# Hybrid diffusion layer on one core: the conditioning product on weights split into high and low parts, with the opening reordered

## What is computed

```python
def mixer_layer(x, mod, rms_g, w_in, b_in, ..., attend):
    shift, scale, gate = jnp.split(mod, 3, axis=-1)
    h = rmsnorm(x, rms_g) * (1 + scale) + shift
    q, k, v, z_a, glu, z_b, gates = jnp.split(h @ w_in + b_in, PROJ_SPLITS, axis=-1)
    ...
# context tokens:  mod = silu(c_ctx) @ w_ada + b_ada
# latent tokens:   mod = silu(c) @ w_ada + b_ada       w_ada is 1024 x 3072
```

## Time and profile before

| what | value |
|---|---|
| median of 3 runs | 1916.28 us (1915.32 to 1918.64) |
| profiled execution, its own time | 1918.94 us |
| profiled execution, span of the core | 1917.1 us |
| TensorE busy | 1861.3 us, 97% of the span |
| VectorE, ScalarE busy | 1018.0 us, 540.8 us |
| first product of `h @ w_in` starts | 45.85 us from the span's start |
| first product of the second chunk starts | 70.45 us |

### The profile page before, as it was taken

The page is one execution under the profiler, slowest core; times in us unless marked ns, Lnnn a source line. Parts: engine busy times, 40 slices in busy tenths (PEclk is TensorE's granted clock), DMA queues, the critical chain, the costliest instruction groups (busy, mean ns, idle before and its releaser), DMA issues.

```text
span 1917.1 us, 27200 instructions
## 1 busy us (share of the span) xinstructions
PE 1861.3 (97%) x10707; PEld 1566.2 (82%) x10707; DVE 1018.0 (53%) x1713; ACT 540.8 (28%) x1053; POOL 123.8 (6%) x221
## 2 busy tenths in 40 slices
PE   7999999999999999999999999989999999999998
PEld 1788899988888888888888888878887888878886
DVE  2554512111188348807852894656667555554444
ACT  2641101021111111211111115656667322221221
POOL 0000000000000000000000014222230000000000
PEclk9999999999999999999999999999999999999999
DMA  8614423143022112202220176878884766573421
GB/s 279 197 58 159 154 72 130 50 140 114 11 90 78 58 39 80 80 28 69 88 69 28 58 169 146 185 157 178 163 164 132 230 206 202 157 256 119 156 99 55
DMA packets 212042, 235.09 MB, mean 123 GB/s; under 512 B 47707, under 2 KB 158155, under 8 KB 208715
## 3 DMA queue, kind: packets, MB, share of 16 engines
q1 hardware_dynamic: 211656, 233.24, 41.7%
q10 hardware_dynamic: 259, 0.11, 0.0%
HBM read 152.52 MB, written 80.78 MB: 122 GB/s over the span
## 4 chain that ended last, share of the span: by engine, by line
PE 88%; DMA 3%; issue 2%; DVE 2%; SPq 2%; ACT 2%; POOL 1%; POOLq 0%; DVEq 0%; ACTq 0%
PE banks L765 17%; PE banks L767 17%; PE banks L766 17%; PE banks L1145 4%; PE banks L1652 3%; PE banks L1654 3%; PE banks L1653 3%; PE banks L1624 3%; PE banks L1626 3%; PE banks L1625 3%; PE banks L1112 2%; PE banks L760 2%; PE banks L761 2%; PE banks L762 2%; PE banks L1117 1%
## 5 line engine op out<-in xcount | busy, mean ns | idle before, releaser
L765 PE MATMUL banks<-h_hi,w_hi 128*128 128x512 f32 (+1 forms) x1600 | 593.0, 371 | 3.1 <-DVE w_lo L550 1.9
L767 PE MATMUL banks<-h_hi,w_lo 128*128 128x512 f32 (+1 forms) x1600 | 589.4, 368 | 0.0
L766 PE MATMUL banks<-h_lo,w_hi 128*128 128x512 f32 (+1 forms) x1600 | 589.2, 368 | 0.0
L706 DVE SCALAR_TENSOR_TENSOR conv_acc<-glu_out,taps,conv_acc 128x773 f32<-128x773 f32 x360 | 371.7, 1032 | 12.2
L765 PEld LDWEIGHTS banks<-h_hi,w_hi 128*128 128x128 f32 x1600 | 302.0, 189 | 56.5 <-DVE w_lo L550 2.8
L767 PEld LDWEIGHTS banks<-h_hi,w_lo 128*128 128x128 f32 x1600 | 301.7, 189 | 50.6
L766 PEld LDWEIGHTS banks<-h_lo,w_hi 128*128 128x128 f32 x1600 | 301.9, 189 | 49.1
L490 ACT ACTIVATE out_stage<-banks,param_cols 128x512 f32<-128x512 f32 (+1 forms) x120 | 77.0, 647 | 442.4 <-PE banks L767 436.3
L1251 ACT ACTIVATE probs<-scores,stat 128x640 f32<-128x640 f32 (+2 forms) x128 | 106.8, 834 | 65.7 <-DVE stat L1176 64.8
L1624 PE MATMUL banks<-y_hi,wp_hi 128*128 128x512 f32 (+1 forms) x320 | 120.8, 377 | 0.6 <-DVE y_lo L1797 0.5
L1626 PE MATMUL banks<-y_hi,wp_lo 128*128 128x512 f32 (+1 forms) x320 | 118.7, 371 | 0.0
(11 more groups left out here) (155 smaller groups left out, 2419.2 us busy)
## 6 DMA issues: line engine op xcount, KB each, us to landing
proj<-out_stage SPq DMA_DIRECT2D x96, 256.0 KB, 2.0
w_raw<-in_w_in SPq DMA_DIRECT2D x44, 512.0 KB, 4.0
gates_in<-proj SPq DMA_DIRECT2D x64, 256.0 KB, 3.1
k_hi<-k_hi_rows SPq DMA_DIRECT2D x16, 640.0 KB, 13.9
k_lo<-k_lo_rows SPq DMA_DIRECT2D x16, 640.0 KB, 16.2
w_ada<-in_w_ada SPq DMA_DIRECT2D x8, 1024.0 KB, 11.2
x_rows<-in_x_sample SPq DMA_DIRECT2D x4, 2048.0 KB, 11.5
x_out<-in_x_sample SPq DMA_DIRECT2D x16, 512.0 KB, 3.7
```

Source lines behind the costliest of these rows:

```text
L706: op = dve.scalar_tensor_tensor(dst, src, tap, dst, ALU.mult, ALU.add)
L765: pe.matmul(out, w_hi[:, s, k], h_hi[c][:, k], start=first, stop=False)
L766: pe.matmul(out, w_hi[:, s, k], h_lo[c][:, k], start=False, stop=False)
L767: op = pe.matmul(out, w_lo[:, s, k], h_hi[c][:, k], start=False, stop=last)
```

## The change

The conditioning product is done on split operands. The 16 quarters of the columns (numbered q = 0 to 15; a quarter is four pieces of 128 rows by 256 columns) are each rounded by ScalarE (`ada_high`) and the remainder is made by VectorE in place (`ada_low`). The stationary operand becomes four columns: the high and the low part of the two vectors (`silu_hl`). Each piece takes two products of 256 columns, one with the high and one with the low part of the weights, both into the same four rows of the result. `turn_row` then folds the four rows into two while it transposes, by a product with a 4x2 matrix `fold` in place of the identity. `row_of` moves from VectorE to ScalarE.

```diff
         load_ada(0)
+        load_x(0)
         load_ada(1)
-        load_x(0)
+        load_w(sp, 0)
         load_ada(2)
-        load_w(sp, 0)
+        load_w(sp, 1)
         load_ada(3)
-        load_w(sp, 1)
         load_w(sp, 2)
         load_x(1)
...
+        def ada_high(q):
+            i, h, kh = q // 4, q // 2 % 2, q % 2
+            act.wait_ge(ada_in[q // 2], 16)
+            if q >= 4:
+                act.wait_ge(ada_done, q - 3)
+            act.activation(wada_hi[:, q % 4], wada[i][:, h, 4 * kh:4 * kh + 4], ACT.Copy).then_inc(ada_hid, 1)
+
+        def row_of(i):
+            act.wait_ge(ada_done, 4 * i + 4)
+            if i >= 2:
+                act.wait_ge(ada_mm, i - 1)
+            act.activation(ada_row[:, i % 2], ps_sum[i % 2], ACT.Copy).then_inc(ada_out, 1)
...
+        def ada_low(q):
+            i, h, k = q // 4, q // 2 % 2, slice(4 * (q % 2), 4 * (q % 2) + 4)
+            dve.wait_ge(ada_hid, q + 1)
+            dve.tensor_tensor(wada_lo[i][:, h, k], wada[i][:, h, k], wada_hi[:, q % 4].bitcast(F32), ALU.subtract).then_inc(ada_lod, 1)
...
-            for kc in kcs:
-                last = pe.matmul(ps_sum[i % 2], sc[:, kc], wada[i][:, :, kc], start=(kc == 0), stop=(kc == KC - 1))
+            for kh in range(2):
+                q = 4 * i + 2 * h + kh
+                pe.wait_ge(ada_lod, q + 1)
+                for k in range(4):
+                    kc = 4 * kh + k
+                    pe.matmul(out, silu_hl[:, kc], wada_hi[:, q % 4, k], start=(kc == 0), stop=False)
+                    last = pe.matmul(out, silu_hl[:, kc], wada_lo[i][:, h, kc], start=False, stop=(kc == KC - 1))
+                last.then_inc(ada_done, 1)
...
+        both(0)
...
+        turn_row(0)
+        pe.wait_ge(cols_out, 2)
+        for s in range(3):
+            turn(s)
+        both(1)
+        turn_row(1)
+        step(0, [0])
+        turn(3)
+        step(1, [0])
+        turn(4)
+        step(2, [0])
+        step(3, [0])
+        both(2)
+        for s in range(4):
+            step(s, [1])
+        turn_row(2)
+        turn(5)
+        ada_products(3, 0)
+        turn(6)
+        step(4, [0, 1])
+        ada_products(3, 1)
+        step(5, [0, 1])
+        turn_row(3)
+        turn(7)
+        for s in range(6):
+            step(s, [2])
+        step(6, [0, 1, 2])
+        step(7, [0, 1])
```

More of the change, by code:

```diff
@@ L490, in evict @@
                 act.activation(ostg[:, s, 0:w], src, func, bias=bias_of(kind, col)).then_inc(ev_act, 1)
+        for q in range(4):
+            ada_high(q)
+        row_of(0)
         squares(0)
+        ada_high(4)
+        ada_high(5)
         high(0)
[L494 to L496 removed]
+        ada_high(6)
+        ada_high(7)
+        modulate(0)
+        modulate(1)
+        row_of(1)
+        ada_high(8)
+        ada_high(9)
+        modulate(2)
+        modulate(3)
+        high(1)
+        ada_high(10)
+        ada_high(11)
+        row_of(2)
+        ada_high(12)
+        ada_high(13)
+        modulate(4)
+        modulate(5)
+        ada_high(14)
+        ada_high(15)
         high(2)
[L498 to L499 removed]
+        row_of(3)
+        modulate(6)
+        modulate(7)
         squares(1)
[L501 removed]
+        s = KC
         for i, upto in enumerate(TURNED_BY):
@@ L578, in front_dve @@
         coefficients(0)
-        row_of(1)
-        coefficients(1)
-        normalize(0)
-        row_of(2)
-        coefficients(2)
[L584 to L588, removed]
+        ada_low(4)
+        normalize(0)
+        ada_low(5)
+        low(0)
+        ada_low(6)
+        ada_low(7)
+        split(0)
+        split(1)
+        coefficients(1)
+        ada_low(8)
+        ada_low(9)
+        split(2)
+        split(3)
+        low(1)
+        ada_low(10)
+        ada_low(11)
+        coefficients(2)
+        ada_low(12)
+        ada_low(13)
+        split(4)
+        split(5)
+        ada_low(14)
+        ada_low(15)
         low(2)
-        split(3)
-        split(4)
         coefficients(3)
-        s = 5
+        split(6)
+        split(7)
+        normalize(1)
+        s = KC
         for i, upto in enumerate(TURNED_BY):
@@ L809, in front_pe, with both @@
                 products(u, i % KC)
+        def both(i):
+            ada_products(i, 0)
+            ada_products(i, 1)
+        both(0)
+        pe.wait_ge(rows_in, 16 * 7)
+        pe.transpose(ps_rows, rows[0:R_C, :], cst.ident[0:R_C, 0:R_C]).then_inc(turned, 1)
+        pe.transpose(ps_taps, taps[0:4 * TAPS, :], cst.ident[0:4 * TAPS, 0:4 * TAPS]).then_inc(turned, 1)
+        turn_row(0)
[26 more added lines that the diff above has]
+        step(7, [0, 1])
+        s = KC
+        for i, upto in enumerate(TURNED_BY):
+            if i < KC - 1:
+                continue
+            while s < upto:
+                turn(s)
+                s += 1
+            if i == KC - 1:
+                step(i, [2])
+            else:
+                step(i, range(3 * (i // KC), 3 * (i // KC) + 3))
         pe.wait_ge(lo_done, len(STEPS))
```

78 lines of the change are left out of this document (30 added, 48 removed).

## The result

| | before | changed |
|---|---|---|
| median | 1917.84 us (1914.42 to 1921.08, 20 runs) | 1921.99 us (1916.61 to 1925.26, 20 runs) |
| ratio, 95% interval | 1 | 1.0023 [1.0016, 1.0029] |
| profiled execution, span (own time) | 1917.1 us (1918.94) | 1919.1 us (1920.85) |
| TensorE busy | 1861.3 us | 1849.9 us |
| first product of `h @ w_in` | 45.85 us | 35.63 us |

The kernel is slower by 0.23% by the ratio (4.4 us on 1917.84), and by 4.15 us between the two medians. TensorE is busy for 11.4 us less and starts the projection 10.2 us sooner, and the second chunk still comes later. Turn 12 is the best mark: by then each queue holds the same instructions in both kernels, and nothing of the opening is left. It starts 76.52 - 72.62 = 3.90 us later.

What follows compares the result with a forecast made beforehand. TensorE bounds the kernel; the change moves only the second chunk's first product. At full clock 14.6 us saved are lost to waits, sum 0; clock terms +4.6, rounded to +4.5, on 1916.3 give 1920.8 us, range 1914.5 to 1926.

Steps and rivals of the forecast that it cites:

- three clock terms: TensorE's low level before turn 0 (+1.5 us), between 33 and 39 (+1.6), before turn 8 (+1.5); sum +4.6.
- Rows at 17.3 and the 5.4 us: Opening transfers: token rows move ahead of 2.1 MB of weights, 5.4 us, and land at 17.3 instead of 22.7.
- Turn 0 at 27.1: Opening on TensorE: factors at 23.5, subtraction 4 ends at 24.3, normalizing takes 2.7 us, so turn 0 at 27.1.
- Four-column products at 0.12 us: TensorE's quarters: 256-column products 0.12 us from start to start, 16 quarters 15.2 us against 29.8 before.
- the subtraction at 1.17: VectorE's 16 subtractions: about 1.17 us each from start to start, 18.7 us more before step 8.
- the plain rate: Rival on TensorE: four-column products take 0.215 us, +9 us, 1925 with the clock on top; chance 0.07.
- a cheap subtraction: Rival on VectorE: subtraction 0.9 us or less, path 2.2 to 2.9 us shorter, 1913.4 to 1914; chance 0.12.
- First product of `h @ w_in` at 34.0: TensorE after VectorE's first gapless run and the row copy: projection starts at 34.0 against 45.85, 11.9 us earlier.
- Quarters 8 to 11, `turn_row(2)`, the run of subtractions: Relay: 32 products end at 43.75, `turn_row(2)` at 46.9, coefficients at 47.3, VectorE's gapless 6.9 us to 54.2.
- Squares of the second chunk at 58.8: ScalarE after the last products, `turn_row(3)`, coefficients and `modulate` 6 and 7: the squares start only at 58.8.
- Point 6: Second chunk: squares to factors 6.2 us, normalized by 67.7; TensorE waits 2.8 for turn 8; step 8 at 70.5.
- `turn_row` 0.4 us: TensorE in the relay: each `turn_row` step takes 0.35 to 0.40 us; the 4x2 `fold` was costed at nothing.

Runs made afterwards that it cites:

- e6: Kernel before with only its transfers reissued in the changed kernel's order, token rows ahead of 2.1 MB of weights; ratio to the kernel before 1.0013.
- e5: Changed kernel with transfers issued in the order of the kernel before, token rows behind the second conditioning weights; one execution, 1926.86 us.
- e4: Changed kernel plus 64 unused products of 256 columns on TensorE between `turn_row(0)` and turn 0; ratio to the kernel before 1.0019.
- e8: Changed kernel with all edits of e7 plus the 64 unused products of e4; ratio to the kernel before 0.9993.
- e2: Changed kernel with evictions of units 0 and 1 moved right behind the second chunk's squares on ScalarE; ratio to the kernel before 1.0007.
- e1: Changed kernel with `turn_row` again four transposes of the first two rows, the vectors' low-part rows left out; ratio to the kernel before 1.0011.
- e7: Changed kernel with both edits of e9, `turn_row` transposing all four rows and VectorE adding the halves; median 1914.39 us, ratio to the kernel before 0.9982.
- e3: Changed kernel with two of the second chunk's four squares before the last row copy and two behind it; ratio to the kernel before 1.0001.
- e9: Changed kernel with the squares moved as in e3 and the evictions as in e2; ratio to the kernel before 1.0000.

## Why the prediction was right, and where it was not

The forecast was 1920.8 us against 1916.28, a ratio of 1.0024, and slower as the likelier sign; measured are 1.0023 and 1921.99 us. The 1916.28 was the median of three runs; over twenty it is 1917.84, so the +4.5 us of the forecast stand against +4.15 between medians. The frame held: the gain of the early start is lost again in a relay over VectorE and ScalarE, and the shift stands before turn 12. That the number came so near is in good part luck: of three clock terms only the first is in the profile, and two terms that the prediction did not have, the fold and the evictions, are as large as the two that are missing.

- *Rows at 17.3 and the 5.4 us.* Held. Squares start at 16.90 right behind the row copy, without a wait for the rows. In e6, where they wait for the rows alone, they start at 16.79 and not 22.71, and e5 shows 5.83 us (22.73), a little more than 5.4.
- *Turn 0 at 27.1.* It came at 26.59 after 8.59 idle us, 0.5 us to the good. With the new order it lies between 26.13 and 27.34 in eight profiles, so the half microsecond is within the scatter.
- *Four-column products at 0.12 us, the subtraction at 1.17.* Both held: 0.12 us apart (33.58 to 33.70), and two subtractions in 2.35 us. The rivals of the plain rate and of a cheap subtraction fall.
- *First product of `h @ w_in` at 34.0, with the clock's 1.5 at 35.5.* Measured 35.63.
- *Quarters 8 to 11, `turn_row(2)`, the run of subtractions.* The run was forecast from 47.3, 48.8 with the clock's term, and measured from 49.22; its 6.9 us were 6.75 (49.22 to 55.97).
- *Squares of the second chunk at 58.8.* With the first clock term 60.3, measured 61.26: the folds (1.7 us) and the larger first clock term (0.3) come on top, and about 1.1 us go off, by which the rest of the path was shorter than forecast. Point 6 then held: 2.58 us of wait for 2.8, and step 8 came 2.71 us after turn 8 (70.16 to 72.87), where the forecast's own terms give about 2.8.
- *The clock, +1.5, +1.6, +1.5.* This is the term that was mis-sized. The first is real and somewhat larger, 1.83 us from turn 0 to `turn_row(1)` (8.06 against 6.23 in e4 and e8; 1.3 to 2.3 over the other executions). The second and third are not in the changed kernel's profile. They are not false either: the stretch at 50 to 55 fell in e2 and e4 and cost 0.75 us there, half of the 1.6, and that at 70 to 75 fell in e1, e2 and e4. They come and go between executions of queues that are alike up to there. The third costs 1.2 us by itself (e2), and nothing where the eviction wait is hidden under it (6.40 us from turn 8 to turn 12 with the one in e1, 6.36 with the other in the changed kernel). A term of "always, +3.1" should have been "sometimes, up to 2, and not on top of other waits".
- *`turn_row` 0.4 us.* The step was read from the transposes of the kernel before and carried over to a product with `fold`, which is another operation: 1.05 us. The prediction put the fold itself at nothing, since the matrix is made early; what it left out is the use of it. The shift of the path is 1.7 us (e1), or 1.5 with the additions that replace it (e7).
- *Evictions.* The prediction did not have them. The three turns 8, 9 and 10 now stand together, and `evict(0)` stands behind `modulate` of these on ScalarE, with a table load of 1.28 us before it. That was 1.3 us (6.30 against 4.99, e3 and e9).

The forecast's own terms at full clock, section by section, beside what was measured:

| section | forecast, full clock | changed kernel | the same without the cause |
|---|---|---|---|
| turn 0 | 27.1 | 26.59 | |
| to `turn_row(1)` | 6.5 | 8.06 | 6.23 without the low stretch (e4, e8) |
| to turn 8 | 34.1 | 35.51 | 33.80 without the fold (e1) |
| to turn 12 | 5.0 | 6.36 | 4.99 without the eviction wait (e9) |
| turn 12 | 72.7 | 76.52 | |

The last 5.0 are the 2.8 from turn 8 to step 8 and the 2.17 that the kernel before takes from step 8 to turn 12. So the forecast's path would have had turn 12 level with the kernel before (72.7 and 72.62), and the 3.9 us are: the first low stretch +1.83, the fold +1.71, the eviction wait +1.37, and about 1.1 us that the rest of the path was shorter than forecast, half of it turn 0. The prediction had 4.6 by three clock terms. The squares are no term of this sum: they are a delay that the full-clock sum already held (point 6), and taking it away pays 2.4 us. The low stretch of the kernel before (50 to 55) is in its 72.62; an execution without it may have an earlier mark, and then the shift is larger than 3.9.

Left open: why behind the mark one program takes between 1838.5 and 1845.4 us in single profiles, and with it how much of the time a shift of 1 us at the mark is. From the changed kernel to e7_all_folded the mark goes down by 5.8 us and the ratio by 0.0041, some 7.9 us; to e8_all_and_filler by 7.2 and some 5.8 us. One for one fits both within that scatter, and no closer.

## What to carry to other kernels

When a product is made cheaper by splitting its operands, lay out the queue of the engines that make the split: here 14.6 us saved on TensorE (by the forecast; its busy time fell by 11.4) were paid by 16 roundings and 16 subtractions, and the price was set by what stood behind them in the same queue (squares, evictions), where moving squares and evictions gave back 3.5 us. A small operation on the relay (a fold, a transpose) costs its whole latency once for each turn of the relay, so it is priced by a row of the same operation, or else bounded. And a shift is measured at a mark from which both programs are alike, in several executions, and section by section: a low stretch that comes or goes (0.75 to 2.3 us here) is as large as an edit (1.3 to 2.7).

## What the runs showed of the hardware

- Four plain float32 products of 4x128 by 4x2 are eight instructions and take 1.05 us; four transposes of four rows are four and take 0.41 us. That is 0.13 and 0.10 us for each instruction: the twofold number of them makes most of the difference.
- The granted clock after short waits is not a function of the queue. The same wait of 1.09 us for a subtraction stands at 50.59 in the changed kernel and at 49.99 in e2_evict_early; the window 50 to 55 has 1.00 in the one and 0.66 in the other. The fall comes in the middle of work, not in the wait: in e4_filler products start 0.12 us apart from 49.32, behind the wait, and 0.21 apart from 50.54 on. Transposes follow the clock as well: twelve took 2.79 us at the low level and 1.50 at the high.
- At the start of the work the spacing tells the level, and the window does not: in the changed kernel products of 256 columns stand 0.21 us apart from 10.78 to 13.34, while the window 10 to 15 is given as 1.00.
- A low stretch can be free: in e1 and e4 the one behind turn 8 took the place of the eviction wait (turn 8 to turn 12: 6.40 and 6.35 us, 6.36 with the wait). Its cost is what it adds beyond the next thing that TensorE would have waited for.
